# Low parts of the activations begin 128 or 64 bytes further on in their tiles

## What is computed

```
def reference(...):
    for i in range(DEPTH):                       # DEPTH = 2
        xn = _rmsnorm(x, norm_gain[i])
        if i % N_MIXERS == 0:
            y = _diff_attention(xn, attn_w_in[j], attn_w_out[j], ...)
        else:
            y = _conformer_conv(xn, conv_w_in[j], conv_b_in[j], conv_dw[j], ...)
        x = x + y
    return _rmsnorm(x, final_gain)

_diff_attention:
    q, k, v, gate = split(xn @ w_in)             # 2048 x 8192
    p = softmax(q k^T + bias[rel])               # two maps a head
    o = headnorm((p[0] - lam * p[1]) @ v)
    return (o * silu(gate)) @ w_out              # 2048 x 2048

_conformer_conv:
    a, g, z = split(xn @ w_in + b_in)            # 2048 x 6144
    u = depthwise_conv31(a * sigmoid(g)) + dw_b
    u = silu(layernorm(u) * ln_g + ln_b)
    return (u * silu(z)) @ w_out + b_out         # 2048 x 2048
```

## Time and profile before

| | us |
|---|---|
| median of 3 runs | 839.0 (838.97 to 844.24) |
| the profiled execution, as timed | 839.93 |
| its span in the profile | 838.1 |
| PE busy in the span | 828.4 (99%) |
| DVE busy | 646.4 (77%) |
| ACT busy | 449.1 (54%) |
| POOL busy | 228.9 (27%) |
| HBM read | 160.76 MB, 196 GB/s over the span |

### The profile page before, as it was taken

The page is one execution under the profiler, slowest core; times in us unless marked ns, Lnnn a source line. Parts: engine busy times, 40 slices in busy tenths (PEclk is TensorE's granted clock), DMA queues, the critical chain, the costliest instruction groups (busy, mean ns, idle before and its releaser), DMA issues.

```text
span 838.1 us, 13848 instructions
## 1 busy us (share of the span) xinstructions
PE 828.4 (99%) x5628; PEld 767.0 (92%) x5628; DVE 646.4 (77%) x1098; ACT 449.1 (54%) x590; POOL 228.9 (27%) x107
## 2 busy tenths in 40 slices
PE   9999999999999999999999999999999999999996
PEld 9998799889998899888888899999999999998885
DVE  7568694697757794798788987999999998566651
ACT  7747444447436454457544465455554556694432
POOL 0300000000000000001000007988899888680000
PEclk9999999999999999999999999999999999999999
DMA  9978547555555457544555556655555555549502
GB/s 329 395 260 282 166 157 233 168 169 176 202 190 171 161 166 233 176 150 151 202 201 189 183 180 205 200 189 178 192 197 191 177 191 197 194 159 350 184 17 101
DMA packets 99665, 163.68 MB, mean 195 GB/s; under 512 B 3600, under 2 KB 40720, under 8 KB 99096
## 3 DMA queue, kind: packets, MB, share of 16 engines
q1 hardware_dynamic: 98128, 160.64, 56.7%
q10 hardware_dynamic: 1480, 2.25, 0.7%
HBM read 160.76 MB, written 3.69 MB: 196 GB/s over the span
## 4 chain that ended last, share of the span: by engine, by line
PE 99%; issue 0%; ACT 0%; POOL 0%; DVE 0%; POOLq 0%
PE ps_acc L1256 17%; PE ps_acc L1255 17%; PE ps_acc L1253 17%; PE ps_acc L1239 14%; PE ps_acc L1241 14%; PE ps_acc L1242 14%; PE ps_acc L1297 1%; PE ps_acc L1301 1%; PE ps_acc L1304 1%; PE ps_a L1347 1%; PE ps_a L1349 1%; PE ps_a L1348 1%; PE ps_d L1354 1%; PE ps_d L1335 0%; PE ps_d L1333 0%; PE ps_d L1334 0%
## 5 line engine op out<-in xcount | busy, mean ns | idle before, releaser
L471 ACT ACTIVATE sb_w_hi<-sb_w_raw 128x2048 fp32r<-128x2048 f32 x139 | 265.3, 1917 | 239.9 <-PE ps_acc L1256 162.5
L443 POOL TENSOR_TENSOR sb_w_lo<-sb_w_raw,sb_w_hi 128x2048 fp32r<-128x2048 f32 x45 | 208.5, 4638 | 400.7 <-ACT sb_w_hi L471 400.7
L820 DVE TENSOR_TENSOR sb_w_lo<-sb_w_raw,sb_w_hi 128x2048 fp32r<-128x2048 f32 x94 | 213.9, 2289 | 99.9 <-ACT sb_w_hi L471 99.5
L1253 PE MATMUL ps_acc<-sb_conv_hi,sb_w_hi 128*128 128x256 f32 x768 | 213.7, 278 | 0.0
L1255 PE MATMUL ps_acc<-sb_conv_lo,sb_w_hi 128*128 128x256 f32 x768 | 212.8, 277 | 0.0
L1256 PE MATMUL ps_acc<-sb_conv_hi,sb_w_lo 128*128 128x256 f32 x768 | 212.7, 277 | 0.0
L1057 DVE SCALAR_TENSOR_TENSOR ps_d<-sb_uT,sb_dwT,ps_d 128x256 f32<-128x256 f32 x480 | 188.9, 482 | 4.5 <-ACT ps_d L701 4.5
L1239 PE MATMUL ps_acc<-sb_w_hi,sb_act_hi 128*128 128x512 f32 x384 | 149.7, 390 | 0.0
L1241 PE MATMUL ps_acc<-sb_w_lo,sb_act_hi 128*128 128x512 f32 x384 | 149.5, 389 | 0.0
L1242 PE MATMUL ps_acc<-sb_w_hi,sb_act_lo 128*128 128x512 f32 x384 | 149.4, 389 | 0.0
L1255 PEld LDWEIGHTS ps_acc<-sb_conv_lo,sb_w_hi 128*128 128x128 f32 x768 | 144.2, 188 | 0.1
(11 more groups left out here) (170 smaller groups left out, 885.6 us busy)
## 6 DMA issues: line engine op xcount, KB each, us to landing
sb_w_raw<-in_attn_w_in SPq DMA_DIRECT2D x59, 1024.0 KB, 5.6
sb_w_raw<-in_conv_w_in SPq DMA_DIRECT2D x64, 512.0 KB, 4.5
sb_w_raw<-in_attn_w_out SPq DMA_DIRECT2D x16, 1024.0 KB, 4.9
sb_w_raw<-in_conv_w_in SPq DMA_DIRECT2D x16, 1024.0 KB, 5.1
sb_w_raw<-in_conv_w_out SPq DMA_DIRECT2D x16, 1024.0 KB, 5.0
sb_w_raw<-in_attn_w_in SPq DMA_DIRECT2D x16, 256.0 KB, 4.5
sb_xs<-in_x SPq DMA_DIRECT2D x2, 1024.0 KB, 13.1
sb_x_in<-in_x_turned SPq DMA_DIRECT2D x15, 128.0 KB, 4.4
```

Source lines behind the costliest of these rows:

```text
L443: pool.tensor_tensor(w_part(w_lo, c), w_raw[c % RING][:], w_part(w_hi, c).bitcast(F32), ALU.subtract).then_inc(lo_ready_pool, 1)
L471: act.activation(w_part(w_hi, c if like is None else like), w_raw[slot][:], ACT.Copy).then_inc(hi_ready, 1)
L820: dve.tensor_tensor(w_part(w_lo, like), w_raw[slot][:], w_part(w_hi, like).bitcast(F32), ALU.subtract).then_inc(lo_ready, 1)
L1253: pe.matmul(into, left_hi, hi[:, kt], start=(kt == 0 and f % 2 == 0), stop=False, skip_group_check=True)
```

## The change

The tiles `act_lo` and `conv_lo` become longer by 128 values (512 bytes in a partition) and are read and written through a view that begins 32 values (128 bytes) into the tile for `act_lo` and 16 values (64 bytes) for `conv_lo`. The high parts stay where they are. Everything that is declared behind these tiles moves by 512 bytes, or by 1024. No instruction is added, removed or moved.

```diff
+ACT_LO_AT, CONV_LO_AT = 32, 16
...
+        def by_tile(room, at):
+            return room[:, at:at + KT * SEQ].rearrange("p (k s) -> p k s", s=SEQ)
...
-            act_lo = sb("act_lo", [P, KT, SEQ], F32R, one)
+            act_lo_room = sb("act_lo", [P, KT * SEQ + W_GAP], F32R, one)
+            act_lo = by_tile(act_lo_room, ACT_LO_AT)
...
-                conv_lo = sb("conv_lo", [P, KT, SEQ], F32R, two)
+                conv_lo_room = sb("conv_lo", [P, KT * SEQ + W_GAP], F32R, two)
+                conv_lo = by_tile(conv_lo_room, CONV_LO_AT)
```

## The result

The changed kernel takes 849.65 us (median of 6 runs, 849.24 to 850.14), the kernel before 838.99 us in the same comparison (837.37 to 844.24): ratio 1.0113, with a 95% interval of 1.0085 to 1.014. It is slower, by a little over 1%, where 836.1 us was forecast and the range ended at 843.0.

A forecast was written before the change was run, and what follows sets the result against it. PE's matmul rhythm was taken to bound the kernel; 2.9 us gained in the turned form, with 0 for the row form and all else, took the median of 839.0 to 836.1 us, range 829.2 to 843.0.

The forecast's parts named there:

- What bounds the kernel: PE, busy 99% of the span; only the rhythm in which it starts its matmuls can move the time much.
- Part 1 and 2: DVE and ACT writing and reading low parts elsewhere, and tiles behind moving by 512 or 1024 bytes: price 0 each.
- Part 3: Turned form, moving operand of L1255, one matmul in three: 2.9 us gained; bounds 8.7 us gained, 7.5 us lost.
- the fast stretch: Conv input behind the transposes, 549.79 to 744.27 us: 113.3 ns a matmul instead of 117.8, 35 chunks in 194.48 us.
- Part 4: Row form, stationary operand of L1242, its load at another distance: price 0, bound 2.8 us over 512 matmuls.
- the settling: First five steps of the conv output projection, row form: 232 ns a step, 5.4 more than the later 226.6.
- The fast rhythm is lost: Rival: conv from 549.79 to 744.27 us slows by 4.44 ns a matmul, 7.5 us, giving 846.5 us; chance 0.12.
- slower by over 1%: Outcome over 847.4 us, said to need the lost fast rhythm and the row form's price together; chance 0.06.
- Nothing: Rival: addresses don't matter, the phase of something else sets the rhythm; time stays at 839.0 us; chance 0.22.
- What would show it: Profile windows: last four conv chunks 21.76 us, or 22.6 if slowed; twelve row chunks 65.27, or 65.8 at full price.

The follow-up runs named there:

- e3: Changed kernel with both tiles still longer by 512 bytes but both low parts starting at 0; 836.64 us, beside 840.09 for the kernel before.
- g1: Kernel before with only the low weights of the row form 128 bytes further on, activations unmoved; 844.25 us, beside 838.84 for the kernel before.

## Why the prediction was wrong, point by point

- *What bounds the kernel.* Right. PE's rhythm is all of it; DVE, ACT and POOL have the busy times of before, and no wait took the place of anything.
- *Part 1 and 2, other places for writes and for the tiles behind.* Right, price 0. For the writes: DVE is busy 646.7 us after and 646.4 before. For the tiles behind: e3 kept the rhythms of all projections.
- *Part 3, the turned form.* This is the step that failed, and in its sign. I took 2.9 us gained, since one matmul in three would stand at a distance other than 64 bytes, which I held for the dear one. The runs show 64 bytes, to either side, to be the only distance with 113.3 ns at all, and only where all three products had it; 0, 32, 96 and 128 bytes gave 117.3 to 120.0, and one product in three at another distance gave 117.8. I had read "slow at 64 either side, not at 0" from the earlier trace rows, and had said myself that the comparison with the row form wasn't clean. It was worse than unclean: 0 is the best place in the row form and the worst in the turned form. What the shift did is the worst bound of that part, the loss of the fast stretch, priced at 7.5 us and measured at 201.89 - 194.48 = 7.4.
- *Part 4, the row form.* A term mis-sized. I took 0 with a bound of 2.8 us (5.4 ns for each of 512 matmuls, from the settling in the earlier trace rows); it measured 13.3 ns for each of the 512 triples, 6.8 us, and the settled state, not the first steps, pays it. The reason given for 0, that the load has the time of 512 columns, didn't hold: with all that time the load's place still cost 13.3 ns, and in g1, where no load was moved, moving a stream cost the same.
- *The rivals.* "The fast rhythm is lost" named the place and the price, and with the row form on top it gave 849.3 against 849.65 measured; I gave it 0.12, and 0.06 to slower by over 1%. That agreement is partly luck: the row form was 4.0 us dearer than its bound, and between the profiled executions 3.5 us were given back, most of them round 94 us, where that of before had the longer wait and the half-clock stretch. "Nothing" would have been 839.0, and the row chunks at 226.6, 231.1 and 233.3 ns, with nothing changed but places in SBUF, refute it. The Trainium skill's page "SBUF — State Buffer", section "Who interferes with whom", says that PE never waits on anyone. Read as "places in SBUF don't matter to PE", that doesn't agree with these traces.
- *Where the chances went wrong.* The fast stretch had been seen only with all three products at one distance, and the row form settled only so. I wrote that as an argument for the rival and gave it a small chance. A state that the trace shows only under one condition, and that a change takes away, deserves more.
- *What would show it.* The windows named did: 22.6 for the last four conv chunks was the value given for the lost rhythm. For the row chunks 65.8 was "the price in full"; it is 66.56.

## What to carry to other kernels

Where PE is the bound and streams float32r operands back to back, the places of the moving and the stationary operand in SBUF, taken modulo 256 bytes here, are worth 2 to 6% of its rhythm. Moving one part alone by 64 or 128 bytes cost time in both forms, by 256 or 512 it cost none in the row form. Moving all operands together by 64 bytes (f4) left the row form as it was, but in its one execution the conv input stayed slow, so such a move has to be timed too. Look for the rhythm in starts per window, since mean durations hide it. Two forms of the same product can want opposite distances. When a stretch can run in two rhythms, one execution says little: it takes several before a rhythm can be put down to an edit.

## What the runs showed of the hardware

- The rhythms come in steps. Matmuls of 512 columns ran at 226.7, 231.1 or 233.3 ns, those of 256 columns at 113.3, 117.8 or 120.0 ns among others, at a granted clock of 1.00. In both forms the dearest is 6.7 ns over the cheapest for each matmul, 20 ns a triple, and the middle one 13.3 ns a triple. The middle one isn't always even within the triple (226.7, 232.4 and 234.3 ns in the attention output of the changed kernel).
- Four transposes (0.36 us) ahead of a stretch turned the kernel before to the fast rhythm in attention rounds 2 to 4 of both profiled executions of that program, and one transpose did not in its one execution; which of the two rhythms follows other interruptions differs from execution to execution. What it is in the four transposes wasn't tried.
- A wait of 1.8 to 2.2 us in the issue of PE at 92 us was in five of 20 profiled executions followed by some 3 us at half clock; in a sixth with 2.2 us it wasn't. Wait and stretch together made 3.3 us of difference.
- Open: whether it is two reads that meet, and which, and why moving a stream alone (g1) costs as much as moving a load alone.
